# A decoder layer with 32 experts on one core: a larger weight ring laid around the attention's buffers, a router on pre-norm sums, a first gather from fp32 rows, and scores in pairs

## The reference

```python
mix = hybrid_mixer(h, w_in, ...)            # softmax(q k^T) of 16 maps of head width 64
h = layer_norm(ALPHA * h + mix, ln1_g, ln1_b)
xatt = memory_cross_attention(h, mem_n, w_mem_q, w_mem_kv, w_mem_o)
h = layer_norm(ALPHA * h + xatt, ln2_g, ln2_b)

logits = xt @ w_router + b_router           # xt = h, (256, 1024) @ (1024, 32)
top_val, top_idx = top_k(logits, 4)
top_w = softmax(top_val)
combine = one_hot-weighted top_w, (256, 32)
for e in range(32):
    hid = clamped_swiglu(xt @ w_mlp1[e] + b_mlp1[e])     # 1024 -> 2048 -> 1024
    y = y + combine[:, e:e+1] * (hid @ w_mlp2[e] + b_mlp2[e])
h = layer_norm(ALPHA * h + y, ln3_g, ln3_b)
```

## Time and profile before

| what | us |
|---|---|
| median of 3 runs (lowest to highest) | 1194.06 (1193.45 to 1195.26) |
| the profiled execution, its own time | 1193.01 |
| its span in the profile | 1191.2 |
| PE, DVE, ACT, POOL busy | 1085.8, 326.1, 261.4, 27.2 |
| mean granted TensorE clock, as a share of 2.4 GHz | 0.992 |
| DMA traffic | 446.01 MB, mean 374 GB/s |

### The profile page before, as it was taken

One profiled execution on the slowest core, in us unless ns is written; L12 is line 12 of the kernel. 1 busy time (PEld: TensorE's weight loads), 2 busy tenths in 40 slices (PEclk: granted clock), 3 DMA queues, 4 the chain that ended last, 5 costly groups with the idle time before them and its releaser, 6 DMA issues.

```text
span 1191.2 us, 16168 instructions
## 1 busy us (share of the span) xinstructions
PE 1085.8 (91%) x6675; PEld 524.6 (44%) x6675; DVE 326.1 (27%) x709; ACT 261.4 (22%) x420; POOL 27.2 (2%) x39
## 2 busy tenths in 40 slices
PE   7899999989999999999988888888888888888895
PEld 5788899853333333333333333333333333333331
DVE  4785686562111121111111111111111111111114
ACT  3565656431111111111111111111111111111110
POOL 4000010020000000000000000000000000000000
PEclk9999999989999999999999999999999999999998
DMA  9844557679999999999999999999999999999994
GB/s 290 273 147 137 200 168 262 250 283 367 427 430 427 426 428 427 427 427 429 429 428 427 430 427 429 429 428 429 428 428 430 427 429 429 427 429 429 427 428 182
DMA packets 48499, 446.01 MB, mean 374 GB/s; under 512 B 4640, under 2 KB 4768, under 8 KB 23792
## 3 DMA queue, kind: packets, MB, share of 16 engines
q1 hardware_dynamic: 46784, 439.80, 89.3%
q0 software_dynamic: 1680, 5.70, 1.7%
HBM read 444.43 MB, written 1.05 MB: 374 GB/s over the span
## 4 chain that ended last, share of the span: by engine, by line
DMA 47%; PE 45%; DVE 3%; ACT 3%; issue 1%; POOL 0%; SPq 0%; DVEq 0%; ACTq 0%
DMA ring<-in_w_mlp 45%; PE bank L839 19%; PE bank L864 6%; PE bank L530 4%; PE bank L531 4%; PE bank L532 4%; PE bank L795 2%; DMA w_raw<-in_w_in 1%; PE bank L786 1%; DVE w_split L1160 1%; PE bank L714 1%; PE bank L698 1%; ACT work L1115 1%; DVE h L1191 1%; ACT v L1131 1%
## 5 line engine op out<-in xcount | busy, mean ns | idle before, releaser
L839 PE MATMUL bank<-ring,work 128*64 128x512 f32 x2048 | 454.1, 594 | 50.2 <-DMA ring<-in_w_mlp 49.5
L839 PEld LDWEIGHTS bank<-ring,work 128*64 128x64 f32 x2048 | 140.0, 136 | 345.2 <-issue 240.1
L864 PE MATMUL bank<-ring,v 128*64 128x512 f32 x1024 | 225.1, 592 | 0.0
L1469 DVE TENSOR_SCALAR v<-bank 128x256 f32<-128x256 f32 x64 | 24.2, 420 | 690.7 <-PE bank L839 690.7
L864 PEld LDWEIGHTS bank<-ring,v 128*64 128x64 f32 x1024 | 71.6, 137 | 132.1 <-issue 129.7
L1127 ACT ACTIVATE v<-v 128x512 f32<-128x512 f32 x32 | 20.1, 629 | 478.1 <-DVE v L1469 478.1
L1160 DVE TENSOR_TENSOR w_split<-w_raw,w_split 128x1024 fp32r<-128x1024 f32 x64 | 76.0, 1221 | 39.3 <-ACT w_split L931 38.7
L931 ACT ACTIVATE w_split<-w_raw 128x1024 fp32r<-128x1024 f32 x64 | 65.7, 1055 | 51.7 <-PE bank L532 35.7
L1133 ACT ACTIVATE work<-bank 128x512 f32<-128x512 f32 x32 | 19.1, 597 | 236.1 <-PE bank L864 236.1
L795 PE MATMUL bank<-work 64*128 64x512 f32 x264 | 65.6, 615 | 0.7 <-ACT work L1133 0.7
L786 PEld LDWEIGHTS bank<-pick,work 128*128 128x128 bf16 x1584 | 48.1, 98 | 24.7 <-issue 24.7
(11 more groups left out here) (200 smaller groups left out, 921.2 us busy)
## 6 DMA issues: line engine op xcount, KB each, us to landing
ring<-in_w_mlp SPq DMA_DIRECT2D x192, 2048.0 KB, 24.0
w_raw<-in_w_in SPq DMA_DIRECT2D x24, 512.0 KB, 6.9
w_raw<-in_w_mem_kv SPq DMA_DIRECT2D x16, 512.0 KB, 4.5
w_raw<-in_w_mix_out SPq DMA_DIRECT2D x8, 512.0 KB, 6.0
w_raw<-in_w_mem_q SPq DMA_DIRECT2D x8, 512.0 KB, 6.8
w_raw<-in_w_mem_o SPq DMA_DIRECT2D x8, 512.0 KB, 4.8
h<-in_x SPq DMA_DIRECT2D x4, 256.0 KB, 5.0
mem_o<-in_mem POOLq DMA_DIRECT2D x2, 512.0 KB, 7.6
```

Of the source, the lines that this page charges most:

```text
L839: mm = pe.matmul(up[n][64 * g:64 * g + SLOTS, :], x_e[:, k, :], slot(at)[:, col:col + 512], start=False, stop=(k == KC - 1))
L864: mm = pe.matmul(ty[64 * g:64 * g + SLOTS, :], hidT[:, P * c + 64 * u:P * c + 64 * u + SLOTS], slot(at)[:, D * c + 512 * g:D * c + 512 * ( ...
L1469: last = dve.tensor_scalar(glu[:, S * n:S * (n + 1)], hid[:, :, 0], LIMIT, None, ALU.min)
```

## The change

**Ring.** Twelve slots (two whole experts, 24 MB) instead of ten. All buffers of the dense part, `h` too, lie in it; what must outlive the start of the experts lies in `live` beside it. The slots rotate two experts at a time for all experts. Slots 0 to 4 are asked for after units 12, 33, 38, 42 and 57; slots 5 to 10 after unit 63; slot 11 (the place of `h`) after the first three pieces of expert 2, when the sum of the experts has been started and the down bias is added.

**Weight units.** Eight raw buffers and six rounded ones; DVE's part overwrites the raw unit (`w_low`). SP asks for unit u when PE has used unit u-8.

**Loads.** POOL issues no DMA any more. SP issues the memory tokens, gains and small tables between the first units; the expert biases (three copies of b_mlp1) after unit 42; b_mlp2 is loaded once (128 KB). `w_router` and copies of the LN2 gains and biases in columns come in another layout.

**Scores.** q is kept dense (`qT`), and two heads are multiplied from partitions 0 to 63 and 64 to 127, into two banks, with their matmuls alternating.

**Router.** PE turns the sums before LN2 (`rT`), three of the four groups in between the matmuls of block 15. The gains are multiplied into the router's weights ahead of time, mean and deviation are applied to the logits. Each tile of 128 tokens is routed by itself. The first gather takes fp32 rows of h with an fp32 pick matrix, 16 matmuls, and the first expert starts on the first half of its features. Starting the sum (alpha * h, L785) and the down biases (L856, L862, once for all experts) are placed inside expert 1's up projection. The three bf16 parts are made behind it, on ACT and DVE.

```diff
-NSLOT = 10
-PLACE = [12, 10, 8, 14, 16, 6, 4, 2, 0, 18]
-EARLY = {35: 1, 58: 1}
-RAW = 6
-SPLIT = 5
+NSLOT = 2 * PIECES
+PLACE = [0, 2, 4, 6, 8, 12, 10, 14, 18, 16, 20, 22]
+EARLY = {12: [0], 33: [1], 38: [2], 42: [3], 57: [4]}
+RAW = 8
+SPLIT = 6
...
-            for u in range(2, UNITS * len(BLOCKS)):
-                if u >= RAW:
-                    sp.wait_ge(low_ready, u - RAW + 1)
+            for u in range(RAW, UNITS * len(BLOCKS)):
+                wait_unit_used(sp, u - RAW)
                 load_unit(u)
...
+                if u == 42:
+                    wait_filled(sp, "oT", 1, 1)
+                    for i in range(3):
+                        sp.dma_start(bias_f[E * i:E * (i + 1), :], a["b_mlp1"][0]).then_inc(bias_in, 16)
...
+            prefetch(range(5, NSLOT - 1))
...
+            load_expert(2, 0, 0, range(3))
+            prefetch([NSLOT - 1])
+            load_expert(2, 0, 0, range(3, PIECES))
+            load_expert(3, 1, 1)
...
-            def score(m):
-                b = bank_for(pe, "S", m)
-                pe.matmul(b[:, 0:P], qz[:, m % 8, 0:P], kT[:, m % 8 // 2, 0:P], start=True, stop=True)
-                pe.matmul(b[:, P:SEG], qz[:, m % 8, P:S], kT[:, m % 8 // 2, :], start=True, stop=True)\
+            def score_pair(m):
+                b = [bank_for(pe, "S", m + i) for i in range(2)]
+                rows = [slice(HD * i, HD * (i + 1)) for i in range(2)]
+                j = m % 8 // 2
+                for i in range(2):
+                    pe.matmul(b[i][:, P:SEG], qT[rows[i], j, P:S], kT[rows[i], j, :], start=True, stop=True)
+                for i in range(2):
+                    pe.matmul(b[i][:, 0:P], qT[rows[i], j, 0:P], kT[rows[i], j, 0:P], start=True, stop=True)\
...
+            def gather_first(t, q):
+                for c in range(4 * q, 4 * q + 4):
+                    at = 2 * P * (c // 2) + c % 2
+                    mm = pe.matmul(banks[3 + 4 * q][:, SLOTS * c:SLOTS * (c + 1)], h[:, t, at:at + 2 * P - 1:2],
+                                   pick_first[:, t, :], start=(t == 0 and c % 4 == 0), stop=(t == 1 and c % 4 == 3))
+                return mm
...
+                    if first and k == 5:
+                        for t in range(NT):
+                            mm = start_sum(t)
+                        mm.then_inc(sum_started, 1)
+                        add_down_bias()
```

734 lines of the change are left out of this document (413 added, 321 removed).

## The result

The changed kernel takes **1185.2 us** (median of 11 runs, 1181.36 to 1190.76) against 1193.94 for the kernel before (11 runs, 1192.94 to 1196.0): a ratio of 0.9928, 95% interval 0.991 to 0.9946. It is faster, but by 8.7 us where 20 were forecast, and outside the forecast's range of 1166 to 1184. The profiled execution took 1189.85 us with a span of 1188.0.

What follows compares the result with a forecast made beforehand. The end was taken as fixed by when the experts' weight stream begins and how many pieces are ahead: 255.4 + 887.1 + 29.3 - 0.4 = 1171.4 us span, 1174 us as time, range 1166 to 1184.

Steps and rivals of the forecast that it cites:

- T: First up matmul of the experts, at 270.37 before: forecast 255.4 from dense part, added transposes and router.
- units 1 to 11: Start of the dense part: 30.3 us at 2.75 a unit, 5.8 less, as moved bias loads let unit 8 land earlier.
- block 15's end to T: Router, from the dense part's last matmul to the first up matmul: 13.5 us, a gain of 7.6, bounds 11 and 18.
- P, piece 189 behind T: Ring stream: third-last piece lands 887.1 us after the first up matmul, 891.5 before; a gain of 4.4.
- tail: After piece 189 lands: 29.3 us, less 0.4 for the loss of L857.
- the dense part's sum: Before the router: 5.8 from the first units plus 3.2 from scores, weight units at 0, makes 9.0 us earlier.
- The clock as a term: Router: the clock falls again; at half, gather and bias cost up to 2.7 us more.
- Rival B: Dense part gains nothing because DVE and ACT set its pace: first up matmul at 264.4, time 1183; chance 0.18.
- Pairs: Scores: two half-height maps run together, eight maps 2.6 us instead of 5.3; with halved q copies 3.2, bounds 1 and 6.
- The bound without gaps: Ring stream: piece 189 lands 884.8 us after the first up matmul if no gaps follow; a gain of 6.7.
- Slower (D): Dense part: weight units come late and each block of four waits; 1195 us and up; chance 0.07.
- as before (E): Whole kernel: no piece gained, pairs not together, router chain as long as before; 1192 us, level; chance 0.05.

Runs made afterwards that it cites:

- the early fold: In the changed kernel, DVE empties the bank of the router's column sums ahead of splitting units 12 to 15: 1186.81 us, ratio 0.9926.
- experiment 3: Changed kernel plus thirteen filler matmuls in PE's waits (output stage and router): 1184.85 us, ratio 0.9914; the changed kernel rerun unaltered: 1188.35 us.
- experiment 1: Changed kernel with DVE emptying the router sums' bank before it splits units 12 to 15: 1186.81 us, ratio 0.9926.
- experiment 2's last two: Changed kernel with score maps of one row half first, then the other: 1193.1 us; with both matmuls of a pair over all 128 rows: 1187.33 us.
- experiment 2: Changed kernel with its pairs of score maps altered: issued map by map 1187.5 us, one row half after the other 1193.1, over all 128 rows 1187.33.
- the full-height run: Changed kernel with both score matmuls of a pair over all 128 rows (result not the layer's): 1187.33 us, ratio 0.9941.
- experiment 4: Changed kernel with ring slots 9 and 10 asked for only with slot 11, behind three reused pieces: 1192.73 us, ratio 0.9976.
- 2's first: Changed kernel with a pair's four score matmuls issued map by map instead of alternating: 1187.5 us, ratio 0.9937.
- experiment 5's second: Changed kernel with the down projection's bias cut to one matmul of 32 columns: 1182.15 us, ratio 0.9898.
- experiment 5's first: Changed kernel with sum start and down bias moved behind expert 2's gather, slot 11 behind four reused pieces: 1189.23 us, ratio 0.9957.

## Where the forecast was right, and where it failed

The span was forecast at 1171.4 and is 1188.0. The miss of 16.6 is 10.5 in T, 4.2 between T and piece 189, and 1.9 in the tail.

| step | forecast | measured | what it is |
|---|---|---|---|
| units 1 to 11 | 30.3 | 31.46 | right in kind, 1.2 short |
| scores begin | 50.3 (56.88 less 5.8 and 0.8) | 55.15; 51.71 with the early fold | a wait that I missed, on the sums' bank; behind it DVE binds all the same |
| eight maps, second group | 2.6 | 2.89 | right |
| output stage | 12.3 | 17.65; 12.80 with fillers | half clock |
| block 15's end to T | 13.5 | 14.21 | right, with the low clock that I had put in |
| P, piece 189 behind T | 887.1 | 891.3; 886.8 with the bias moved | first reused piece 2.6 late, gaps of 5.8, not 2.3 |
| tail | 28.9 | 30.8; 29.1 at full clock | half clock in the last down projection |

**T.** The failed step is the dense part's sum, "9.0 earlier". At block 7's end 5.05 were there, and nothing at block 8. The largest term is one that the sum put at nothing: the clock in the output stage, 4.85 us (experiment 3). Of the 3.95 missing at block 7's end, 1.5 are missing at the end of unit 11 already (4.3 won there, not 5.8), 1.3 are the clock's fall in the scores (experiment 1), and about 1.1 are left for DVE, which has the sums' bank and the memory rows' banks to empty before all maps of the first group can run. I read what DVE has to do before units 8 to 11, and not which bank the new matmul takes and who stands behind it; but taking that one wait away showed no gain, since the next one, on DVE as well, ends at the same time. The rest of the 10.5: 0.5 in the output stage with fillers, 0.5 from the half clock's reach into block 8, and 0.7 in the router.

**The clock as a term.** I had it in the router, where the kernel before shows it, and held it at 1.00 everywhere else because the kernel before does. That was the mistake: in the output stage PE meets the same waits (1.1 and 0.7 us, in both kernels), and in the changed kernel the clock fell there in some executions and not in others. Why it falls there now and not in the kernel before stays open. The two kernels whose maps do not run in pairs (experiment 2's last two) did not have the fall either, but that is one profile each. The Trainium skill (TensorE: Matmul & The Clock Gate, Part 1: The HAM clock gate) says that the monitor behind the gate runs freely and isn't restarted with the kernel; the two groups of times of one program agree with that, but no run here shows the monitor itself. Rival B (the dense part gains nothing, 1183) gave nearly the right time, for another reason in the main: DVE costs about 1.1 us at the first group of maps, and the larger loss is the clock's.

**Pairs.** That half-height matmuls run together was right, and so was the time of a group. What they bring to block 7's end was under-sized: 4.2 us (experiment 2) where the sum had 3.2 with the copies of q. In the second group, where I took the chain not to run over PE, they bring 1.9. The rule of the Trainium skill weighed in the prediction (a change of tiling mode drains TensorE) shows as a small cost at most, and not each time: PE is idle for 0.30 us behind the second group (112.19 to 112.49), and has no such gap in the full-height run, but neither has it one behind the first group of the changed kernel (the next matmul starts at 58.95, the last map ends at 59.02), nor behind the second group of the run with one head at a time. It took none of the gain that mattered.

**The ring.** The step "T + 887.1" had the right mechanism: slot 11 behind the bias, and a gap at the first down piece. Its sizes failed. The first reused piece was to land at T + 11.4 and lands at T + 14.0 (asked for at T + 5.1 and not 3.7, and 8.9 us of landing and not 7.7). That is 2.6 us; the gaps behind it are 5.8 and not 2.3, and the pace gives 2.0 back: 4.2 in all. The up projection was to end at T + 22.3 and ends at T + 25.2, the fifth reused piece to be asked for at T + 30.8 and is at T + 35.4. Three stretches at half clock lie in it: until 268.8, from 285.9 (16 matmuls in 5.30 us, where 3.65 is their time at full clock) and from 296.1. The value for the pieces ahead, one place of the stream each, holds only without gaps (experiment 4). The pace was right: 4.896 us a piece for 4.907. The bound without gaps, T + 884.8, is near the run with hardly a bias, T + 886.1, in part by luck: there too the stream starts 2.9 us later than I had it (T + 14.3), and the pace gives 2.0 back.

**Slower (D), or as before (E).** The weight units came in time: PE works 31.08 of 31.46 us in units 1 to 11, and the first ring piece, ahead of unit 13's transfer, costs ACT a wait and PE none. E is not it either: pairs run and the pieces ahead are there.

## What to carry to other kernels

Where an edit makes PE earlier, look at the next place where PE waits: a gain can vanish there by a fall of the clock, in some runs only, and a filler that fits the wait can keep it. Before a gain of 1 or 2 us is put down to an edit, compare the clock of the stretch in both profiles, or find a run with the same lists there; size the filler by a row of the same form, since matmuls on one half of the array run alone. When a new job takes a PSUM bank, follow that bank to its next user and ask what the engine that empties it has in its list before, and which wait stands behind this one. More prefetch is worth its pieces only if the first reused slots are released at the pace of the stream, so move work that can wait out of the stretch that releases them and into a wait behind it.

## What the runs showed of the hardware

- Executions of one program differ by 5 us and more, and the shorter ones have the higher mean granted clock (1181.4 us at 0.988, 1190.8 at 0.979). In six profiles (the changed kernel twice, experiments 1, 2's first, 4 and 5's second) it falls between 127.0 and 129.2 us; in experiment 5's first, with the same lists up to there and block 7 ending at 124.46, it does not. In the scores, lists that are the same have it at 53.8 (the changed kernel) or not at all (experiment 5's second), 1.3 us apart.
- The clock also falls while PE is busy (5.78 of the 6.2 us before it): at 255.2, in the row of narrow logits matmuls behind block 15. With two fp32 fillers of 512 columns among them the low stretch was 255.7 to 266.0 instead of 255.2 to 268.8, and those from 286 and from 296 did not come. That the fillers did this is not shown: without any in the router, the full-height run has a low stretch of the same length (255.7 to 266.0), and the run with hardly a bias has none behind 267.8.
- Matmuls on different halves of the rows overlap without alternating strictly: issued two and two they take about as long as one and one (2.99 and 2.89 us for eight maps), and four and four they take 4.95.
- Fillers that all write one half of the output take 0.90 us each (3.58 for four), where sixteen passes of the up projection, on both halves, take 3.65.
